# Order of TensorE work at the item boundary of a mixture-of-experts loop

## The reference, cut to what matters

```python
logits = jnp.dot(h, w_router) + b_router            # 32 experts, the best 4 for each token
top_logit, top_idx = lax.top_k(logits, TOP_K)
gates = jax.nn.softmax(top_logit, axis=-1)
...
def expert_block(args):                             # xb: rows of tokens of one expert
    xb, e = args
    g = jnp.minimum(xb @ w_gate[e] + b_gate[e], SWIGLU_LIMIT)
    u = jnp.clip(xb @ w_up[e] + b_up[e], -SWIGLU_LIMIT, SWIGLU_LIMIT)
    act = g * jax.nn.sigmoid(SWIGLU_ALPHA * g) * (u + 1)
    return act @ w_down[e] + b_down[e]
...
y_pairs = ys[dest] * pair_gate[:, None]
return jnp.zeros_like(h).at[pair_tok].add(y_pairs)
```

## Time and profile before

| what | value |
|---|---|
| median of 3 runs | 2590.35 us (2585.87 to 2596.69) |
| the profiled execution | 2590.09 us, its span 2588.5 us |
| TensorE matmul busy | 2472.1 us, 96% of the span |
| VectorE, ScalarE, GpSimd busy | 45%, 14%, 10% of the span |
| DMA | 728.36 MB, mean 281 GB/s over the span |
| mean granted clock of TensorE | 0.991 |

### The profile page before, as it was taken

The page is one execution under the profiler, slowest core; times in us unless marked ns, Lnnn a source line. Parts: engine busy times, 40 slices in busy tenths (PEclk is TensorE's granted clock), DMA queues, the critical chain, the costliest instruction groups (busy, mean ns, idle before and its releaser), DMA issues. The chain is left out here.

```text
span 2588.5 us, 34558 instructions
## 1 busy us (share of the span) xinstructions
PE 2472.1 (96%) x13181; PEld 1551.1 (60%) x13182; DVE 1170.5 (45%) x2368; ACT 373.6 (14%) x759; POOL 268.3 (10%) x128
## 2 busy tenths in 40 slices
PE   7999999999999999999999999999999999999998
PEld 3654333333333333337888868777886995676984
DVE  2732221122121221124484258747996666354566
ACT  2322111111111111111113110011001100132000
POOL 0002222222222222210000000000010000000000
PEclk9999999999999999999999999999999999999999
DMA  9548999999997999996535269754997643314451
GB/s 361 222 180 324 418 428 427 428 427 428 428 427 298 407 429 427 428 415 249 204 130 186 107 235 342 277 185 147 366 378 263 227 162 130 137 67 153 163 194 49
DMA packets 191134, 728.36 MB, mean 281 GB/s; under 512 B 9808, under 2 KB 103342, under 8 KB 163286
## 3 DMA queue, kind: packets, MB, share of 16 engines
q1 hardware_dynamic: 171432, 651.31, 64.3%
q0 software_dynamic: 19632, 76.09, 7.4%
HBM read 726.31 MB, written 1.05 MB: 281 GB/s over the span
## 5 line engine op out<-in xcount | busy, mean ns | idle before, releaser
L1679 PE MATMUL bank<-first_raw,experts_xs 128*64 128x512 f32 x2112 | 481.1, 603 | 45.1 <-issue 45.1
L1679 PEld LDWEIGHTS bank<-first_raw,experts_xs 128*64 128x64 f32 x2112 | 150.2, 138 | 343.7 <-issue 339.9
L1832 DVE COPY tiled_spread<-bank 128x256 f32<-128x256 f32 x33 | 14.0, 425 | 691.2 <-PE bank L1712 691.2
L1574 POOL COPY first_raw<-ring 128x4096 f32<-128x4096 f32 x62 | 223.2, 3601 | 905.5 <-DMA ring<-in_w_gate 649.2
L1679 PE MATMUL bank<-first_raw,tiled_act_s 128*64 128x512 f32 x1056 | 238.0, 592 | 1.4 <-DVE tiled_act_s L1871 1.4
L1997 PE MATMUL bank<-hT,ring 128*128 128x256 f32 x1024 | 225.8, 383 | 1.1 <-ACT hT L437 1.1
L1997 PEld LDWEIGHTS bank<-hT,ring 128*128 128x128 f32 x1024 | 196.5, 192 | 30.5 <-issue 3.6
L2469 PEld LDWEIGHTS bank<-hT,big 128*128 128x128 f32 x1408 | 162.1, 192 | 11.6 <-issue 11.6
L1679 PEld LDWEIGHTS bank<-first_raw,tiled_act_s 128*64 128x64 f32 x1056 | 78.2, 137 | 149.7 <-issue 149.7
L2469 PE MATMUL bank<-hT,big 128*128 128x128 f32 x1408 | 164.7, 275 | 2.1 <-DVE hT L477 2.1
L2594 PE MATMUL bank<-big,ffn_actT 128*128 128x512 f32 x352 | 154.7, 592 | 0.0
(11 more groups left out here) (513 smaller groups left out, 2942.2 us busy)
## 6 DMA issues: line engine op xcount, KB each, us to landing
first_raw<-in_w_up SPq DMA_DIRECT2D x64, 2048.0 KB, 14.8
first_raw<-in_w_down SPq DMA_DIRECT2D x64, 2048.0 KB, 16.1
ring<-in_w_gate SPq DMA_DIRECT2D x62, 2048.0 KB, 21.2
big<-in_ffn_w_gu SPq DMA_DIRECT2D x88, 1024.0 KB, 7.8
ring<-in_mod_w POOLq DMA_DIRECT2D x30, 2048.0 KB, 10.9
big<-in_ffn_w_down SPq DMA_DIRECT2D x44, 1024.0 KB, 5.8
ring<-in_w_in SPq DMA_DIRECT2D x16, 2048.0 KB, 8.4
first_raw<-in_w_mod SPq DMA_DIRECT2D x19, 1024.0 KB, 5.8
```

What stands on the lines that cost most here:

```text
L1574: return self.nc.gpsimd.tensor_copy(self.raw[q].rearrange("p k n -> p (k n)"), self.ring[:, q, :])
L1679: last = nc.tensor.matmul(bank[b][h * HALF:(h + 1) * HALF, :], stationary(kt), raw[p][:, k, h * C:(h + 1) * C], start=kt == 0, stop=kt == ...
L1832: vec.tensor_copy(spread[:], bank[X][:, 0:SEQ]).then_inc(spread_ready, 1)
```

## The change

The transposes of `gated` (spreading) move from behind up to ahead of it, and go to bank Y, the bank of the down product, which ScalarE has copied out by then (`y_copied`). TensorE's own wait for `spread_ready` ahead of turn x is gone; scatter keeps its wait. The last spreading, behind the loop, stays in bank X. The number of the expert of item e-1 is loaded behind gate q0 and no longer beside the other one ahead of it. On VectorE `take_spread` reads the bank that it is given; its place in the order is the same.

```diff
-            def spreading(e, x_free, count):
+            def spreading(e, b, free, count):
                 after(pe, gated_ready, e + 1)
-                after(pe, x_free, count)
+                after(pe, free, count)
                 for t in range(TT):
-                    last = nc.tensor.transpose(bank[X][:, t * P:(t + 1) * P], gated[:, t, :], core.ident[:])
+                    last = nc.tensor.transpose(bank[b][:, t * P:(t + 1) * P], gated[:, t, :], core.ident[:])
                 last.then_inc(spread_done, 1)
...
-                expert, last = expert_at(pe, e), expert_at(pe, e - 1)
+                expert = expert_at(pe, e)
                 for q in range(PARTS):
                     gate(e, expert, q)
                     if q == 0:
+                        last = expert_at(pe, e - 1)
                         after(pe, act_ready, e)
                     down(last, q)
                 gather(e + 1)
                 turn(e + 1, g_rows, g_copied, G, g_turned)
+                spreading(e - 1, Y, y_copied, e)
                 up(e, expert)
-                spreading(e - 1, x_copied, e + 1)
-                after(pe, spread_ready, e)
                 turn(e + 1, x_rows, x_copied, X, x_turned)
                 turn(e + 1, u_rows, u_copied, U, u_turned)
                 scatter(e - 1)
             n = number(pe)
-            spreading(n - 1, xs_ready, n)
+            spreading(n - 1, X, xs_ready, n)
...
-            def take_spread(e):
+            def take_spread(e, b):
                 after(dve, spread_done, e + 1)
-                vec.tensor_copy(spread[:], bank[X][:, 0:SEQ]).then_inc(spread_ready, 1)
+                vec.tensor_copy(spread[:], bank[b][:, 0:SEQ]).then_inc(spread_ready, 1)
...
                 if not first:
-                    take_spread(e - 1)
+                    take_spread(e - 1, Y)
...
-            take_spread(number(dve) - 1)
+            take_spread(number(dve) - 1, X)
```

## The result

| | before | changed |
|---|---|---|
| median | 2587.3 us (8 runs, 2584.7 to 2596.69) | 2572.9 us (8 runs, 2567.6 to 2577.3) |
| ratio, 95% interval | | 0.994 (0.9928 to 0.9952) |
| the profiled execution | 2590.09 us, span 2588.5 | 2570.1 us, span 2568.4 |

The changed kernel is 15.5 us faster by the ratio (12.4 to 18.6). It was timed twice more beside other kernels: 0.9956 (0.994 to 0.9971) and 0.9963 (0.995 to 0.9976), 11.4 and 9.6 us. The three together say about 12 us, just under 0.5%. The forecast was 14.1 us, just past the 0.5% that was called measurable; the first comparison lies past it, the two others and the mean of the three short of it.

What follows compares the result with a forecast made beforehand. The loop was taken to run at the pace of its weight loads, 29.41 us an item; start 0.4, double expert 6.7, the item behind it 0.3 and end 6.7 sum to 14.1 us, from 2590.09 to 2576.0, range 2572 to 2586.

Steps and rivals of the forecast that it cites:

- the end: From the last gate copy's end to the last down product: 26.7 us against 33.43, a gain of 6.7 us.
- the two decisive items: In the double expert and at the loop's end, TensorE waits for weights; each was to gain 6.7 us.
- the term at the start: At the loop's first items: 0.85 us of lost DMA time less 0.44 for delayed up, a gain of 0.4 us.
- the double expert: The expert with two items: the next expert's up is requested at 835.9 instead of 842.59, 6.7 us earlier.
- The item: TensorE's time for one loop item while catching up: 27.2 us instead of 28.59, against 29.41 of the loads.
- The wait at turn u: Behind up, turn u has to wait for u_rows: 0.3 us idle, bounds 0.1 and 0.5.
- The register load: Loading the second expert number behind gate q0 is hidden by queued matmuls: cost 0, bounds 0 and 0.6 us.
- What is late next: In caught-up items down q0's load binds, landing 1.3 us after the copy's end; gate q0 starts 3.5 us earlier.
- The rival with the clock: A half-clock stretch in the double expert or last item costs 1.7 us: 2577.7, two 2579.4; chance 0.25.
- Slower: The wait behind gate q0 drops the clock in every item, two drops costing 3.4 us: 2606; chance 0.04.
- catch up by the end: Behind the double expert TensorE makes up 15.4 us in 7 of 11 items; rival that it doesn't: 2580, chance 0.13.
- tied to the gate copies by xs: Rival: gate q0 stays 2.7 to 4.2 us behind the gate copies; 2583 to 2586; chance 0.12.

Runs made afterwards that it cites:

- e5: The changed kernel without the scatter matmuls in the loop, its waits kept; 0.9952, 12.4 us faster than before.
- e9: The changed kernel with 5 matmuls on constants between gate q0 and down q0; 0.9964, 9.3 us faster than before.
- e6: The changed kernel with 12 matmuls on constants between gate q0 and down q0; 1.0107, 27.7 us slower than before.
- e1: The kernel of before with the move of spreading alone, both register loads still ahead of gate q0; 0.9952, 12.4 us faster than before.
- e8: The changed kernel timed again, beside others on one chip; 0.9956, 11.4 us faster than before.
- e3: The changed kernel with spreading into bank X instead of Y, turn x waiting for its copy; 0.9946, 14 us faster than before.
- e2: The kernel of before with only the second expert number loaded behind gate q0; 0.9981, 4.9 us faster than before.
- e4: The changed kernel with both gate halves ahead of both down halves; 0.9923, 19.9 us faster than before.
- e7: The changed kernel with both gate halves, then spreading, gather and turn g, ahead of both down halves; 0.994, 15.5 us faster than before.
- e10: The kernel of e4 timed again, beside the changed kernel on one chip; 0.9936, 16.6 us faster than before.

## Where the prediction held, and the step that failed

**The step that failed.** The mechanism held, and a term of the sum was mis-sized: the end, put at 6.7 us and measured at 5.4. The sum took every half of the weights in the two decisive items at full clock, and put the clock fall aside as a rival with a chance of 0.25. Behind the new wait ahead of down q0 the clock did fall in the last item but one, in all three profiles of the changed kernel. With it the total falls short of the 0.5% that the forecast said would be passed. The first comparison's 15.5 us don't repair this; in its profile the term at the start, 0.4 forecast and 2.4 measured, happened to lie off the other way. That the errors nearly cancel (15.7 for 14.1) is luck.

**The base.** The sum was taken from one profiled execution of before, 2590.09 us, which was 2.8 us slower than the median of eight. A forecast of 2576.0 from it is a gain of 11.3 us on that median, near the 11.4 and 9.6 of the two later comparisons. How much of the 2.8 us are the two clock falls in that trace, at the start and in the double expert, one profile of before can't tell. So the missing 2 us have two possible sources, the clock at the end and the base, and the runs don't part them.

**The bound.** Right. The loads keep 29.41 us an item before and after, 60 us less work changes nothing (e5), 47 us more changes nothing (e9), and an item of 29.9 us costs its excess (e6).

**The item.** 26.88 measured for 27.2. The wait at turn u, for which I took 0.3 with bounds 0.1 and 0.5, came out as 0.2: turn x starts at 287.31, turn u at 288.08, 0.77 behind it, where 0.59 lay between them before (611.43, 612.02). The register load costs nothing behind gate q0, the lower bound. That a load ahead of gate q0 would leave idle time with two of them was wrong (e1), and changed nothing.

**What is late next.** Right: down q0's landing, 1.15 us behind the second copy's normal end (781.55 + 3.60 = 785.15, down at 786.30), for which 1.3 was taken. The place of gate q0 was not: the prediction set it 3.5 us ahead of down q0, 2.2 ahead of the copy's end, and left out the wait of 2.2 us that stands between the two. Caught up, it starts 4.8 us ahead of that end (1118.76 against 1119.98 + 3.60 = 1123.58), and its own gate half was home only 0.1 us before (1115.06 + 3.60 = 1118.66), not 2 us or more. This changed no term, since down's landing still comes last.

**The double expert.** 7.1 us for 6.7 in the profile. The wait in the second item (2.31 us) is where the chain was said to hang. Without the fall of the clock in the first item before, nothing would be different, as the landing binds after the change; but before would be 1.7 us quicker. e8 shows the fall in the second item: 5.5 us then. So the term is 4 to 7 by the clock, not 6.7.

**The end.** 5.4 for 6.7. The rival with the clock is what happened: down q0 at 1124.73 took 5.35 instead of 3.65 behind a wait of 2.32 us. It had been given 0.25 for either place. Part by part, from the copy's end: 1.15 us to down q0 (1.3 forecast), from there to the end of up 1146.52 - 1124.73 = 21.79 (20.3 forecast), and 5.05 to the last down product (5.1 forecast). The whole error is in the middle part. The clock fell there in all three profiles of the changed kernel, and in e1 and e3 too. The wait had been made 2.3 us long in one piece in the caught-up items that don't follow a fall; before, 2.0 us stood ahead of gate q0 and 0.52 ahead of turn x. With the fall in the sum the forecast would have been 14.1 - 1.7 = 12.4 us, which is about what the three comparisons give together. Without it the term would be 7.1.

**The start.** 2.4 for 0.4. Most of it is a clock fall. In the profile of before the clock fell under the first gate half, in that of the changed kernel not. First before, then changed, TensorE's timeline:

```profile
237.91 6.43 PE L1679 MATMUL bank<-first_raw,experts_xs 128*64 128x512 f32 x16
```

```profile
236.92 3.65 PE L1679 MATMUL bank<-first_raw,experts_xs 128*64 128x512 f32 x16
```

e2, in the order of before and without the fall, loses nothing at the start (248.39 to 277.81, 29.42 us). The changed kernel without it is 0.2 above that (29.59), the 0.44 of the later up release in part. With the fall before loses 31.09 - 29.41 + 0.85 = 2.5 us, e1 1.8, e3 4.3 (247.39 to 281.14). Why e3 loses 2.5 more than e1, with up requested 0.4 later, wasn't settled. Whether the fall is chance isn't either: none of the three profiles of the changed kernel has it, nor have e2, e6 and e9; the one profile of before has it, and so have e1, e3, e4, e5, e7 and e10.

**The other rivals.** Slower did not happen: no item had two falls, and single ones were covered by the slack. TensorE did catch up by the end: the waits for down's load are back at 1007.07, seven items behind the double expert, as the sum had it. It is not tied to the gate copies by xs.

**Chances.** 0.50 for faster by over 0.5% and 0.45 for less describe a result of about 12 us well. The sum's place just past the bound rested on leaving out the clock and on the slow execution that it started from.

## What to carry to other kernels

In a loop that runs at the pace of its loads, find the few places where the loads stand still, and cost an edit only in the chain that leads to the next request there, and in the chain behind the last landing. Work in other items is free up to the length of the loads (28.3 us free, 29.9 not, at 29.4), so look at the order of work instead: what needs no late load goes ahead of what does (e4). In these runs waits of 0.7 and 1.5 us (e4, e10) and of 1.0 us (e9) in caught-up items kept the clock; the same wait in one piece of 2.3 us often let it fall. One profile of each side overstated this change by a third or more (20.0 us against 15.5 and 12), in part through clock falls in places that the change doesn't touch. And look where the profiled execution lies among the timed ones before a forecast is added up from it.

## What the runs showed of the hardware

VectorE's last product (two inputs in SBUF, line 1871) took 3.97 us instead of 0.69 while GpSimd's copy ran, and the product ahead of it, under way when that copy began, stretched the copy from 3.60 to 3.97. From the timeline of the changed kernel:

```profile
781.37 0.69 DVE L1868 SCALAR_TENSOR_TENSOR tiled_up<-tiled_up,tiled_gate 128x512 f32<-128x512 f32 x1
781.55 3.97 POOL L1574 COPY first_raw<-ring 128x4096 f32<-128x4096 f32 x1 [1.31 <-DMA ring<-in_w_gate]
...
782.09 3.97 DVE L1871 TENSOR_TENSOR tiled_act_s<-tiled_up,tiled_sig 128x512 f32<-128x512 f32 x1
```

The Trainium skill says so ("SBUF — State Buffer", SBUF: two separate sides): an operation of VectorE with two SBUF inputs and a GpSimd one that reads SBUF exclude each other, whichever starts first. This trace agrees in both directions. In the changed kernel act_ready thus comes at 786.06, 0.24 us ahead of down q0. It was nearly the binding wait, and e3 waits for it 6 times, 4.1 us in all, against 3 times in the changed kernel.

TensorE's granted clock fell to 0.50 behind some of the long waits and not behind others. In the three profiles of the changed kernel 39 waits ahead of down q0 are 2.06 to 2.33 us long, and behind 22 of them it fell; no wait of 0.6 to 0.8 us there was followed by a fall. In the profile of before it fell behind 3 of the 7 waits of about 2.0 us ahead of gate q0. In e4 and e10, whose waits in caught-up items are 0.70 and 1.54 us, none fell there. Why it fell behind one and not behind the next isn't shown.
